# Two-layer hybrid encoder trunk: bonus and lora products moved among the Gram products of the recurrent stage, transposes alone in its levels, and the bonus's keys summed over both directions first

## The reference

```python
def rwkv7_step(state, inp):
    r, w, k, v, kk, a = inp
    sa = jnp.einsum('...vk,...k->...v', state, -kk)
    state = (state * w[..., None, :] + sa[..., :, None] * (kk * a)[..., None, :]
             + v[..., :, None] * k[..., None, :])
    y = jnp.einsum('...vk,...k->...v', state, r)
    return state, y
...
    w_log = -jax.nn.softplus(-(w0 + jnp.einsum('btdr,drc->btdc', wl, w2))) - 0.5
    decay = jnp.exp(-jnp.exp(w_log.astype(jnp.float32)))
    a = jax.nn.sigmoid(a0 + jnp.einsum('btdr,drc->btdc', al.reshape(bsz, seq, 2, ICLR_LORA), a2))
    k_dir = k[:, :, None, :] * (1.0 + (a - 1.0) * k_a)
...
    _, ys = lax.scan(rwkv7_step, state0, xs)
    y = ys[:, 0] + jnp.flip(ys[:, 1], axis=0)
    bonus = jnp.sum(rh[:, :, None] * kh * r_k, axis=(2, 4))
    out = (y + bonus[..., None] * vh).reshape(bsz, seq, RWKV_WIDTH)
    return out * g
```

## Time and profile before

| | us |
|---|---|
| median of 3 runs | 1762.81 (1762.13 to 1765.85) |
| profiled execution | 1760.1 |
| its span, first to last instruction | 1758.3 |
| TensorE busy | 1690.9, 96% of the span |
| VectorE busy | 1043.1, 59% |
| ScalarE busy | 815.1, 46% |
| GpSimd busy | 448.2, 25% |
| granted TensorE clock | 0.998 of full speed |
| recurrent stage, first Gram product of pair 0 to the chain step behind pair 3 | 156.09 to 346.53, 190.4 |

### The profile page before, as it was taken

The page is one execution under the profiler, slowest core; times in us unless marked ns, Lnnn a source line. Parts: engine busy times, 40 slices in busy tenths (PEclk is TensorE's granted clock), DMA queues, the critical chain, the costliest instruction groups (busy, mean ns, idle before and its releaser), DMA issues.

```text
span 1758.3 us, 29729 instructions
## 1 busy us (share of the span) xinstructions
PE 1690.9 (96%) x12805; PEld 1381.5 (79%) x12805; DVE 1043.1 (59%) x1308; ACT 815.1 (46%) x1235; POOL 448.2 (25%) x405
## 2 busy tenths in 40 slices
PE   7999888899999999999999999999999999999999
PEld 6877777678888787888877886668887787788877
DVE  5478677356243566766676445975434455675667
ACT  5244545536553433543345236865654343353343
POOL 2002222130100472245310220540010166114620
PEclk9999999999999999999999999999999999999999
DMA  7210000143222565375443222003431275356623
GB/s 253 85 48 2 4 4 28 51 168 120 96 96 72 195 236 180 119 247 185 162 167 107 94 74 72 1 1 120 144 111 43 89 271 189 125 198 233 211 98 140
DMA packets 116926, 212.70 MB, mean 121 GB/s; under 512 B 4248, under 2 KB 50939, under 8 KB 116795
## 3 DMA queue, kind: packets, MB, share of 16 engines
q1 hardware_dynamic: 103239, 159.59, 27.2%
q0 software_dynamic: 13264, 51.09, 8.1%
q10 hardware_dynamic: 291, 0.12, 0.0%
HBM read 185.62 MB, written 25.17 MB: 120 GB/s over the span
## 4 chain that ended last, share of the span: by engine, by line
PE 71%; DVE 11%; ACT 8%; issue 4%; POOL 4%; DMA 3%; DVEq 0%; ACTq 0%; POOLq 0%
PE PS L431 47%; PE PS L538 10%; POOL DW L671 2%; DVE WLO L397 2%; ACT WHI L386 2%; PE PS L1922 1%; DVE SS L2225 1%; DMA diff_dn<-DW 1%; PE PS L1891 1%; PE PS L937 1%; DVE CV L2028 1%; DVE CG L2028 1%; DVE CV L2025 1%; DVE CG L2025 1%; ACT CV L2003 1%
## 5 line engine op out<-in xcount | busy, mean ns | idle before, releaser
L397 DVE TENSOR_TENSOR WLO<-WRAW,WHI 128x2048 fp32r<-128x2048 f32 (+1 forms) x106 | 248.0, 2350 | 296.8 <-ACT WHI L386 296.8
L431 PE MATMUL PS<-HIS,WHI 128*128 128x512 f32 x856 | 335.0, 391 | 5.0 <-DVE CV L2028 1.8
L431 PE MATMUL PS<-HIS,WLO 128*128 128x512 f32 x856 | 333.2, 389 | 0.0
L431 PE MATMUL PS<-LOS,WHI 128*128 128x512 f32 x856 | 333.1, 389 | 0.0
L386 ACT ACTIVATE WHI<-WRAW 128x2048 fp32r<-128x2048 f32 (+1 forms) x107 | 203.2, 1907 | 230.3 <-PE PS L431 182.9
L431 PE MATMUL PS<-WHI,HIS 128*128 128x512 f32 x608 | 240.1, 395 | 0.2 <-DVE LOS L728 0.2
L431 PE MATMUL PS<-WLO,HIS 128*128 128x512 f32 x608 | 237.0, 390 | 0.0
L431 PE MATMUL PS<-WHI,LOS 128*128 128x512 f32 x608 | 236.6, 389 | 0.0
L431 PEld LDWEIGHTS PS<-HIS,WHI 128*128 128x128 f32 x856 | 160.6, 188 | 42.4 <-DVE CV L2028 4.0
L431 PEld LDWEIGHTS PS<-HIS,WLO 128*128 128x128 f32 x856 | 160.7, 188 | 33.7
L431 PEld LDWEIGHTS PS<-LOS,WHI 128*128 128x128 f32 x856 | 160.7, 188 | 33.2 <-issue 0.2
(11 more groups left out here) (331 smaller groups left out, 2838.5 us busy)
## 6 DMA issues: line engine op xcount, KB each, us to landing
WRAW<-ffn_w_up SPq DMA_DIRECT2D x88, 512.0 KB, 5.0
RW<-ffn_w_down POOLq DMA_DIRECT2D x22, 1024.0 KB, 7.4
diff_dn<-DW POOLq DMA_DIRECT2D x22, 1024.0 KB, 5.3
WRAW<-cross_wkv SPq DMA_DIRECT2D x16, 1024.0 KB, 5.0
PW<-diff_dn SPq DMA_DIRECT2D x8, 1536.0 KB, 9.1
WRAW<-diff_w_in SPq DMA_DIRECT2D x12, 1024.0 KB, 5.2
WRAW<-ab_w_in SPq DMA_DIRECT2D x10, 1024.0 KB, 5.7
PW<-diff_dn SPq DMA_DIRECT2D x8, 1280.0 KB, 7.6
```

The lines of the kernel that those rows point to most:

```text
L397: V.e.tensor_tensor(part(WLO[place(i)], i), part(WRAW[raw_slot[i]], i), part(WHI[place(i)], i).bitcast(F32), ALU.subtract).then_inc(S("w_l ...
L431: mm = e.matmul(o, l, r, start=(si == 0 and kk == 0 and q == 0), stop=(si == len(steps) - 1 and kk == nk - 1 and q == 2))
```

## The change

In the recurrent stage:

- The bonus operand is made of the sum of both directions' keys (an add of 512 columns, a wait for it, a product of 512 columns), so the bonus is one matmul and not two. The two operations and the KAP product form a function of their own, `prep_bonus_dve`.
- The bonus product and both lora products of the next pair leave the side steps and go into `gram_pe`, through banks 2 and 3: first lora behind the A group (after the QT copies of the pair before, `p_qfree`), bonus ahead of the first KAP group (after the first tanh pair), second lora ahead of the second KAP group (after the copy BON). ScalarE does the tanh pair, the copy BON and the second tanh pair at the start of `pair_act`. The level-0 product of direction 1 waits until bank 2 is free.
- The side steps: BET transposes at s = 2, KAP at s = 4, AR at s = 6, the values' product at s = 8 as before; the odd steps are empty, but for the gates of the last pair at s = 3 and 5.
- `prep_exp_act` moves from s = 7 to s = 5. VectorE's scan, key, scale and bonus preparations stand in levels 1, 2, 3 and 4. The four gating subtractions of pair 0 move from level 1 to levels 0 and 2.

```diff
@@ gram_pe @@
         mm.then_inc(S("p_a"), 1)
+        if j > 0:
+            e.wait_ge(S("p_qfree"), j)
+        if j + 1 < NJ:
+            lora_pe(e, j + 1, 0, 2)
 
         for l, d, b in ((BET, 0, 6), (BET, 1, 0), (KAP, 0, 4), (KAP, 1, 6)):
+            if (l, d) == (KAP, 0):
+                bonus_pe(e, j)
+            elif (l, d) == (KAP, 1) and j + 1 < NJ:
+                e.wait_ge(S("p_bonfree"), j + 1)
+                lora_pe(e, j + 1, 1, 2)
@@ new @@
+    def bonus_pe(e, j):
+        e.wait_ge(S("p_bonus"), j + 1)
+        if j + 1 < NJ:
+            e.wait_ge(S("p_lorafree"), 2 * j + 3)
+        e.matmul(PS[:, 2, :], rk("bones"), TMP[1][:, 0, :], start=True, stop=True).then_inc(S("p_bonmm"), 1)
@@ side_pe @@
-        if s == 2:
-            e.wait_ge(S("p_gfree"), 2 * (j + 1))
-            e.wait_ge(S("p_bonus"), j + 1)
+        if s in (3, 5) and j + 1 == NJ:
+            e.wait_ge(S("p_tokfree"), 3 * j + s // 2)
+            gates_pe(e, s - 3)
+        elif s in (2, 4):
+            if s == 2:
+                e.wait_ge(S("p_gfree"), 2 * (j + 1))
+            else:
+                e.wait_ge(S("p_tokfree"), 3 * j + 1)
...
             for d in range(2):
-                mm = e.matmul(PS[:, 6, :], rk("bones"), TMP[1][:, d, :], start=(d == 0), stop=(d == 1))
-            mm.then_inc(S("p_bonmm"), 1)
...
+                for t in range(NT):
+                    mm = e.transpose(PS[:, 6 + d, t * P:t * P + P], (BET, KAP)[s // 2 - 1][:, d, t * P:t * P + P], ident)
+            mm.then_inc(S("p_tok"), 1)
+        elif s == 6:
+            e.wait_ge(S("p_tokfree"), 3 * j + 2)
@@ pair_pe @@
-                if lv == 0 and d == 1 and j > 0:
-                    e.wait_ge(S("p_qfree"), j)
+                if lv == 0 and d == 1:
+                    e.wait_ge(*((S("p_lorafree"), 2 * j + 4) if j + 1 < NJ else (S("p_bonfree"), NJ)))
@@ side_act @@
-        elif s in (3, 4):
-            if j + 1 < NJ:
-                prep_tanh_act(e, j + 1, s - 3, 6)
...
+        elif s == 5:
+            prep_exp_act(e, j + 1)
@@ pair_act @@
+        if j + 1 < NJ:
+            prep_tanh_act(e, j + 1, 0, 2)
+        e.wait_ge(S("p_bonmm"), j + 1)
+        e.activation(BON[j][:, :], PS[:, 2, :], ACT.Copy).then_inc(S("p_bonfree"), 1)
+        if j + 1 < NJ:
+            prep_tanh_act(e, j + 1, 1, 2)
@@ prep_bonus_dve @@
-        e.scalar_tensor_tensor(TMP[1][:, :, :], TMP[3][:, :, :], col("rwkv_r_k", j), r, ALU.mult, ALU.mult)\
+        V.mine(e.tensor_tensor(TMP[1][:, 0, :], TMP[3][:, 0, :], TMP[3][:, 1, :], ALU.add))
+        V.wait_mine()
+        e.scalar_tensor_tensor(TMP[1][:, 0, :], TMP[1][:, 0, :], col("rwkv_r_k", j), ZS[ZR + j][:, :], ALU.mult, ALU.mult)\
             .then_inc(S("p_bonus"), 1)
@@ pair_dve @@
-            elif j == 0 and lv == 1:
-                for g in range(SGU_G):
-                    sgu_low_dve(e, g)
+            if j == 0 and lv in (0, 2):
+                sgu_low_dve(e, lv)
+                sgu_low_dve(e, lv + 1)
...
-            if j + 1 < NJ and lv >= 2:
-                (prep_scan_dve, prep_key_dve, prep_scale_dve)[lv - 2](V, j + 1)
+            if j + 1 < NJ and lv >= 1:
+                (prep_scan_dve, prep_key_dve, prep_scale_dve, prep_bonus_dve)[lv - 1](V, j + 1)
```

More of the change, by code:

```diff
@@ L1052, in rw0_dve @@
         prep_scale_dve(V, 0)
+        prep_bonus_dve(V, 0)
     def zv_act(A):
@@ L1265, in side_pe @@
         e = T.e
-        if s == 2:
-            e.wait_ge(S("p_gfree"), 2 * (j + 1))
-            e.wait_ge(S("p_bonus"), j + 1)
-            for d in range(2):
-                mm = e.matmul(PS[:, 6, :], rk("bones"), TMP[1][:, d, :], start=(d == 0), stop=(d == 1))
-            mm.then_inc(S("p_bonmm"), 1)
-        elif s == 3:
-            e.wait_ge(S("p_bonfree"), j + 1)
-            if j + 1 < NJ:
[L1275 to L1289, removed]
+        if s in (3, 5) and j + 1 == NJ:
[6 more added lines that the diff above has]
+                e.wait_ge(S("p_tokfree"), 3 * j + 1)
+                if j + 1 == NJ:
+                    e.wait_ge(S("f_gg"), 2)
+                    e.wait_ge(S("f_bg"), 2)
+            for d in range(2):
+                for t in range(NT):
[3 more added lines that the diff above has]
+            e.wait_ge(S("p_tokfree"), 3 * j + 2)
+            if j + 1 == NJ:
                 e.wait_ge(S("f_gg"), NJ)
@@ L1302, in side_pe @@
                                           KC[half(1), HD:P], start=True, stop=True)
[L1303 to L1308, removed]
             mm.then_inc(S("p_tok"), 1)
@@ L1507, in side_act @@
             fin_square_act(e, 1)
-        elif s == 2:
-            e.wait_ge(S("p_bonmm"), j + 1)
-            e.activation(BON[j][:, :], PS[:, 6, :], ACT.Copy).then_inc(S("p_bonfree"), 1)
-        elif s in (3, 4):
-            if j + 1 < NJ:
-                prep_tanh_act(e, j + 1, s - 3, 6)
[L1514 to L1518, removed]
-            for d in range(2):
[L1520 to L1526, removed]
+        elif s in (3, 5) and j + 1 == NJ:
+            fin_gate_act(e, s - 3)
+            fin_gate_act(e, s - 2)
+        elif s in (2, 4):
+            e.wait_ge(S("p_tok"), 3 * j + s // 2)
+            for d in range(2):
+                if s == 2:
                     i = e.activation(units(GB[:, d, :, CH:P]), PS[:, 6 + d, :].rearrange("p (t b k) -> p b t k", b=2, k=HD),
@@ L1531, in side_act @@
             i.then_inc(S("p_tokfree"), 1)
[L1532 to L1536, removed]
+        elif s == 5:
+            prep_exp_act(e, j + 1)
+        elif s == 6:
+            e.wait_ge(S("p_tok"), 3 * j + 3)
+            for d in range(2):
+                i = e.activation(units(AXT[:, d, :, 0:HD]),
+                                 banks2(6, d * 256, 256).rearrange("p b (t k) -> p b t k", k=HD), ACT.Copy)
+            i.then_inc(S("p_tokfree"), 1)
+        elif s == 7 and j + 1 == NJ:
+            e.wait_ge(S("p_bet"), NJ)
+            hi_part(A)
         elif s == 9 and j + 1 == NJ:
@@ L1626, in prep_scale_dve, with prep_bonus_dve @@
             e.scalar_tensor_tensor(ecl(d, j), own, 0.0, own, ALU.mult, ALU.add)
+    def prep_bonus_dve(V, j):
+        e = V.e
+        r = both(ZS[ZR + j][:, :])
         e.wait_ge(S("p_e"), 2 * j + 2)
         if j > 0:
-            e.wait_ge(S("p_tok"), 3 * j)
+            e.wait_ge(S("p_tok"), 3 * j - 1)
         e.tensor_tensor(KAP[:, :, :], TMP[3][:, :, :], TMP[2][:, :, :], ALU.mult).then_inc(S("p_fm"), 1)
         e.wait_ge(S("p_bk"), j + 1)
-        e.scalar_tensor_tensor(TMP[1][:, :, :], TMP[3][:, :, :], col("rwkv_r_k", j), r, ALU.mult, ALU.mult)\
+        V.mine(e.tensor_tensor(TMP[1][:, 0, :], TMP[3][:, 0, :], TMP[3][:, 1, :], ALU.add))
+        V.wait_mine()
+        e.scalar_tensor_tensor(TMP[1][:, 0, :], TMP[1][:, 0, :], col("rwkv_r_k", j), ZS[ZR + j][:, :], ALU.mult, ALU.mult)\
             .then_inc(S("p_bonus"), 1)
@@ L1643, in beta_pool @@
         if j > 0:
-            e.wait_ge(S("p_tok"), 3 * j - 1)
+            e.wait_ge(S("p_tok"), 3 * j - 2)
         e.tensor_tensor(BET[:, :, :], both(KK[:, j, :]), TMP[1][:, :, :], ALU.mult).then_inc(S("p_bk"), 1)
```

## The result

The changed kernel takes 1765.78 us (median of 12 executions, 1763.92 to 1768.55); the kernel before, measured in turn with it, 1762.10 (12, 1760.70 to 1766.21). The ratio is 1.0018, 95% interval 1.0010 to 1.0026: 3.2 us slower by the ratio, where 4.0 us faster was forecast. The profiled execution has a span of 1762.9 us for 1758.3.

What follows compares the result with a forecast made beforehand. TensorE's own order of work was taken to bound the levels. Levels -13.6, Gram products +8.8, masks +0.3, supply +1.0, weight loads -0.5 gave -4.0 us: 1756.1 profiled, 1758.8 median, range 1754.5 to 1765.8.

Steps and rivals of the forecast that it cites:

- The Gram products: Gram stretches, all pairs: two lora products, one bonus product and new waits delay the level-0 products, +8.8 us together.
- Gram cover: Rival, Gram products: long products let supply catch up and stalls vanish, or QT clears sooner; -7 us, 1755.8, chance 0.17.
- The levels: Levels 1 to 4: products and transposes leave, exponentials move; -3.6, -4.1, -4.1, -1.8 us in pairs 0 to 3, -13.6 together.
- two XX masks of level 2 end at +8.1 and +8.7 ... I take 0.1 per pair: Level 2: masks queue behind GpSimd's BET product and the scans; TT products want them at +7.8 and +8.7; 0.1 us per pair.
- TensorE waits in level 2 for XX: Sign that the forecast is wrong; it expected no wait for XX above 0.3 us.
- the mask is late: Rival: level 1's scan or chain update starts one GpSimd product (2.36 us) later, pairs 0 to 2; +3 us, 1765.8, chance 0.18.
- weight loads that miss the dense stretch: Pair 3: weight loads, released three us earlier in their level, no longer stretch the instruction supply; -0.5 us.
- whatever is taken out shortens the stage until a copy on ScalarE is waited for: Premise for the levels, where TensorE's own order of work was said to set the time.
- 0.25 per pair, between nothing and the whole 1.0: Tails: part of the last levels' gain comes back as instruction-supply stalls; 0.25 us per pair, +1.0 in the sum.
- the prediction named at most 0.5: Sign for the tails: stalls that no engine ends at most 0.5 us longer.
- The two supply terms: Instruction supply: +1.0 us for stalls in the tails, -0.5 us for pair 3's weight loads.
- supply decides: Rival: the levels give back what levels 3 and 4 win, another 2.5 us over four pairs; -1.5, 1761.3, chance 0.22.

Runs made afterwards that it cites:

- gate_late: Changed kernel with pair 0's four gating subtractions on VectorE in level 4, not levels 0 and 2: 1763.78 us, ratio 1.0003 to the kernel before.
- shift_only: Changed kernel with four useless products, 16 columns wide, ahead of TensorE's waits for masked XX in pair 0: 1760.55 us, ratio 0.9993 to the kernel before.
- shift12: Changed kernel with twelve narrow useless products in pair 0 (three, six and three in levels 1 to 3): ratio 1.0037 to the kernel before.
- before_again: Second profile of the kernel before, unchanged: 1762.55 us, recurrent stage 193.19 us for 190.44 the first time.
- bonus_tail: gate_late with the bonus product of pairs 1 to 3 moved into the tail of the pair before: 1760.13 us, ratio 0.9992 to the kernel before.
- fewer: Changed kernel without the tails' products of transposed KAP with the values (128 instructions per pair): 1754.10 us, one execution.
- fewer_before: Kernel before without the tails' products of transposed KAP with the values: 1751.62 us, one execution.
- shift12_before: Kernel before with the same twelve narrow useless products in pair 0 as shift12: ratio 1.0020 to the unshifted kernel before.

## Why the prediction was wrong

**The Gram products: right in pairs 0 to 2, by luck in pair 3.** +8.8 us forecast for the start of the level-0 products, +9.0 measured (+3.6, +3.0, +2.6, -0.1 for +3.4, +2.5, +2.3, +0.6); up to the first transposes of level 1 it is +7.5. The bonus of pair 0 did stand for the tanh, QT's copy held pair 2's first lora product by only 0.24 us, and no bonus waited in pairs 1 and 2. The bonus took 1.05 us to the next product for the 0.86 reckoned. Pair 3 is shorter because its stall measured 1.18 us for 2.79, a piece of the rival "Gram cover" that the forecast left out; pair 1's stall is 1.79 us as before.

**The levels: the cuts were right, but stalls and late masks took half of them.** -13.6 forecast, -6.2 measured. Pair 1 shows the working as it was meant: levels of 5.3, 5.7, 5.9 and 4.0 us for 5.4, 5.4, 5.7 and 4.0, in sum -3.8 for -4.1. Of the 7.4 us that lack, 0.3 are pair 1's; the rows name most of the rest:
- pair 0, 2.0 us (-1.7 for -3.6): the masks, and the fall of the clock behind them. The levels took 5.4, 6.3, 7.7 and 4.1 us for 5.3, 5.3, 6.9 and 4.0. The step "two XX masks of level 2 end at +8.1 and +8.7 ... I take 0.1 per pair" was mis-sized there. The gating subtractions, which the diff moves ahead of level 1's and level 3's masks, were not reckoned at all. They meet GpSimd's sum, and the scaling behind them meets its product for BET. It is the named sign of being wrong, "TensorE waits in level 2 for XX", 1.62 us for at most 0.3. It is also the mechanism of the rival "the mask is late", but in one pair of four; in pairs 1 and 2 TensorE waited for no mask. gate_late shows this part. That the rival's time, 1765.8 us, is the one measured is luck: it had 7 us for pairs 0 to 2 where this took about 2.
- pair 2, 2.3 us: stalls of 0.98 and 0.61 us inside the levels, 0.45 for the chain's update of YL behind the scans (pair 1 has it too; the sum has 0.1 per pair for lateness there), and small change.
- pair 3, 2.9 us: a stall of 2.14 us among the products of values (L1321) while weights load, and a part of a fall of the clock. The forecast had -0.5 for weight loads that miss the dense stretch. The tail is 2.9 us shorter, but level 4 is 2.5 us longer (6.78 us for 4.26), so in sum the two give -0.3; the stall moved into the level, where the sum had none.

**Instruction supply: the step that failed.** The premise "whatever is taken out shortens the stage until a copy on ScalarE is waited for" left no room for stalls in levels 1 to 4; the sum had the supply in the tails alone, "0.25 per pair, between nothing and the whole 1.0". A constant at one place was the wrong form. By the rows the stalls moved:

| stalls, us | before | changed |
|---|---|---|
| Gram products and level 0 | 6.5 | 3.0 |
| levels 1 to 4 | none | 3.7 |
| tails of pairs 0 to 2 | 3.9 | 7.1 |
| tail of pair 3 | 3.8 | 1.0 |

The tails of pairs 0 to 2 grew by 3.4 us (0.9, 1.6, 0.9). Their stalls are 1.1, 1.4 and 0.6 us longer, where the prediction named at most 0.5. The two supply terms, +1.0 and -0.5, agree with the sum of all stalls (14.9 us for 14.3), but only because what the levels and tails got, the Gram products and pair 3's tail lost: that is luck, and in the second profiles the sums are 12.8 and 14.5. And shift_only and shift12, the same kernel shifted by 16 and 48 instructions, are 4.4 us faster and 3.3 us slower. The rival "supply decides" named the mechanism at 1761.3 us, but as a give-back in the tails. A forecast that doesn't know the place of the stream carries an uncertainty of that size.

**The clock: not in the prediction.** The mean granted clock is 0.0013 lower than before, worth 1.5 us by the fit above. A fit doesn't show that the change lowered it. Every fall in the stage in the four profiles of these two kernels stands behind gaps of 0.8 to 2.5 us; that such gaps don't always bring one is shown by before_again. What settles a fall stays open, and with it how the 3.2 us divide between masks, place and clock.

**Outside the stage.** Between the two profiles 2.9 us arise behind the stage, which I had taken as unchanged. 1.0 us comes at the start of cross-attention (TensorE waits 1.40 us for LOS at 426.66 for 0.36 us before; the loads of cross_wq landed in 6.0 us for 5.0), 1.7 us in the last products at 1715 us, where the clock falls in most profiles here and not in before's first one. before_again has that fall too. None of it is in the part that the change edits; why the loads landed later stays open.

## What to carry to other kernels

Where TensorE runs many products of 64x64, count instructions and not only time: in a stretch with stalls a long product can be nearly free (bonus_tail), and many short ones can cost more than they last (fewer). An effect of a few us there must be measured at several places of the stream, with a few useless narrow products ahead in both versions, before it is believed. When an edit moves VectorE work across a level, list what GpSimd does at that moment: here the price was 2.36 us for 1.28 and 2.78 for 0.81.

## What the runs showed of the hardware

**Blocks of instructions.** Windows of the changed kernel between the stalls at 243.41, 247.23 and 250.68 us, and, of the DMA queues over 240 to 252 us, the one that brings instructions (packets, MB, share):

```profile
243.41:247.23 3.82, 2.90 (x128) 2.76 (x128) 2.17 (x4) 0.00 (x0) 0.00 (x0) 1.00 0.02 4
247.23:250.68 3.45, 2.09 (x128) 1.96 (x128) 0.41 (x1) 0.60 (x1) 2.90 (x4) 1.00 0.03 7
```

```profile
q8 instruction: 4, 0.07, 2.2%
```

From stall to stall there are 128 matmuls and 128 weight loads, 256 instructions, with 2.9 and 2.1 us of work in 3.8 and 3.5 us. shift12 has the same between its stalls at 198.60, 202.33 and 206.06 us (3.73 us each, with one weight load more in the second). The Trainium skill (Runtime: NRT & Kernel Launch, "Instruction fetch mechanics") says that instructions are refilled in blocks of 256, and this trace agrees. The same section of the Trainium skill calls the cost of crossing a block's boundary mostly hidden; here it isn't: the stalls at these three places are 1.16, 0.92 and 1.36 us long.

**The clock in so full a kernel.** TensorE is busy 96% of the span, and yet its granted clock falls to 1.2 GHz for a few us, at one to six places in a profile (one in fewer_before, six in shift12_before), and not at the same ones each time. The falls in the stage that the two kernels show stand behind gaps of 0.8 to 2.5 us; a wait of 2.38 us in the last products at 1714 us brought none in before's first profile and one of 2.37 us did in the changed kernel's.
